# Tap matmuls on quarters of the array and half of the E transposes moved in a decoder trunk kernel

## The reference

```
h = x + 1/2 * SwiGLU_1(norm(x))
z = norm(h) @ W_in            # 2048 columns: 1536 for the conv heads, 512 for the S5 heads
y_a = B * causal_depthwise_conv3(C * v)
y_s = GLU(Re(C_bar state) + D * u_s)   # 32 channel groups of 16, a 64-dim complex diagonal state each
h = h + W_out(concat[norm(y_a), norm(y_s)])
h = h + 1/2 * SwiGLU_2(norm(h))
h = h + (p @ W_ple) * sigmoid(norm(h) @ W_gate)
```

```
kc[32*s + c_in, b, c_out] = sum over states of Er[state, b, s, c_in] * Gr[state, b, 0, c_out] + Ei * Gi
```

## Time and profile before

| | |
|---|---|
| median of 3 runs | 1042.67 us |
| the runs | 1042.33, 1049.44, 1042.67 us |
| profiled execution | 1048.33 us |
| its span, first to last instruction | 1046.5 us |
| its mean granted TensorE clock | 0.991 |
| busy: TensorE, VectorE, ScalarE, GpSimd | 1032.0, 658.3, 523.5, 364.6 us |
| tap matmuls (L1564, L1565) | 128 instructions in two layers |
| transposes of E (L1660) | 64 instructions in two layers |

### The profile page before, as it was taken

How to read it: one execution, slowest core, us unless ns; L and a number is a source line. 1 busy time by engine, 2 the same in 40 slices (tenths; PEclk the granted TensorE clock), 3 DMA queues, 4 the chain that set the end, 5 groups by cost and what they waited for, 6 DMA issues and landing times.

```text
span 1046.5 us, 15114 instructions
## 1 busy us (share of the span) xinstructions
PE 1032.0 (99%) x5345; PEld 882.1 (84%) x5345; DVE 658.3 (63%) x776; ACT 523.5 (50%) x736; POOL 364.6 (35%) x573
## 2 busy tenths in 40 slices
PE   8999999999999999999999999999999999999996
PEld 6888888899988888888788888889999888888885
DVE  5555665689876546655767545545897855455465
ACT  5544444575754444444664444444667444434454
POOL 6888999600137889940019400001002000000001
PEclk9999999999999999999999999997999999999999
DMA  9865555423457755553646655551334466556541
GB/s 278 247 197 174 191 191 172 160 81 130 145 165 187 260 174 187 189 197 136 201 162 200 200 181 181 199 188 54 121 122 161 157 207 198 185 177 199 189 150 44
DMA packets 143419, 181.56 MB, mean 173 GB/s; under 512 B 18384, under 2 KB 125584, under 8 KB 143376
## 3 DMA queue, kind: packets, MB, share of 16 engines
q1 hardware_dynamic: 143088, 180.48, 52.5%
q10 hardware_dynamic: 288, 0.52, 0.1%
HBM read 179.93 MB, written 1.05 MB: 173 GB/s over the span
## 4 chain that ended last, share of the span: by engine, by line
PE 97%; DVE 1%; ACT 1%; issue 0%; POOL 0%; POOLq 0%; ACTq 0%; DVEq 0%
PE ps L1426 29%; PE ps L1428 29%; PE ps L1427 29%; PE ps L1549 2%; PE ps L1443 1%; PE ps L1565 1%; PE ps L1564 1%; PE ps L1682 1%; PE ps L1696 1%; PE ps L1695 1%; PE ps L1681 1%; PE ps L1694 1%; PE ps L1660 1%; DVE wL L786 0%; ACT wH L419 0%
## 5 line engine op out<-in xcount | busy, mean ns | idle before, releaser
L786 DVE TENSOR_TENSOR wL<-raw,wH 128x1024 fp32r<-128x1024 f32 x336 | 423.5, 1302 | 129.3 <-ACT wH L419 129.2
L419 ACT ACTIVATE wH<-raw 128x1024 fp32r<-128x1024 f32 x336 | 335.9, 1052 | 126.2 <-PE ps L1428 121.6
L1426 PE MATMUL ps<-wH,uH 128*128 128x512 f32 x832 | 329.9, 396 | 3.7 <-DVE wL L786 2.5
L1428 PE MATMUL ps<-wH,uL 128*128 128x512 f32 x832 | 324.5, 390 | 0.0
L1427 PE MATMUL ps<-wL,uH 128*128 128x512 f32 x832 | 324.1, 390 | 0.0
L1426 PEld LDWEIGHTS ps<-wH,uH 128*128 128x128 f32 x832 | 156.3, 188 | 36.9 <-DVE uL L813 3.1
L1428 PEld LDWEIGHTS ps<-wH,uL 128*128 128x128 f32 x832 | 156.2, 188 | 33.3
L1427 PEld LDWEIGHTS ps<-wL,uH 128*128 128x128 f32 x832 | 156.5, 188 | 30.4
L1426 PE MATMUL ps<-wH,hTH 128*128 128x512 f32 x352 | 137.7, 391 | 0.0
L1428 PE MATMUL ps<-wH,hTL 128*128 128x512 f32 x352 | 137.4, 390 | 0.0
L1427 PE MATMUL ps<-wL,hTH 128*128 128x512 f32 x352 | 137.0, 389 | 0.0
(11 more groups left out here) (177 smaller groups left out, 1175.7 us busy)
## 6 DMA issues: line engine op xcount, KB each, us to landing
raw<-in_ffn_w_down_dram SPq DMA_DIRECT2D x88, 512.0 KB, 3.9
raw<-in_ffn_w_gate_dram SPq DMA_DIRECT2D x86, 512.0 KB, 4.0
raw<-in_ffn_w_up_dram SPq DMA_DIRECT2D x86, 512.0 KB, 5.0
raw<-in_w_in_dram SPq DMA_DIRECT2D x32, 512.0 KB, 4.3
raw<-in_w_out_dram SPq DMA_DIRECT2D x16, 512.0 KB, 4.2
raw<-in_ple_w_gate_dram SPq DMA_DIRECT2D x16, 512.0 KB, 4.0
raw<-in_glu_w_dram SPq DMA_DIRECT2D x4, 512.0 KB, 3.7
raw<-in_ple_w_proj_dram SPq DMA_DIRECT2D x4, 512.0 KB, 3.7
```

Source lines behind the costliest of these rows:

```text
L419: nc.scalar.activation(wH[:, slot, w], raw[:, slot, w], ACT.Copy).then_inc(wh_done, 1)
L786: nc.vector.tensor_tensor(wL[:, slot, w], raw[:, slot, w], wH[:, slot, w].bitcast(F32), ALU.subtract).then_inc((wl_half, wl_done)[a], 1)
L1426: mul(o, sH, vH, start=start, stop=False)
L1428: return mul(o, sL, vH, start=False, stop=stop)
```

## The change

1. The taps are computed with the operands swapped. `tap_round` makes G (32 columns) the stationary tile and streams the 128 columns of E. The output of block b = 4r + j goes to partitions 32j to 32j + 31 of PSUM bank 0, columns 128r to 128r + 127, so four matmuls in a row use four different quarters of 32 columns of the array. ScalarE copies the 512 columns to `kc` (semaphores `kt_ps`, `kt_done`), four transposes (`turn_taps`) turn them into bank 1, and ScalarE copies them to `kc` again, now in the layout that the rest of the kernel uses.
2. The turned E uses banks 6, 7, 2, 3. Two of the four groups of Er are turned ahead of x's tile 1, two behind it, and all 16 transposes of Ei come behind W_in unit 0.
3. W_in units 0 and 1 wait for the two copies of the taps (banks 0 and 1) instead of the E copies.
4. VectorE writes the second half of the low part of U_IN+1 after the norm, and the gains of tile 1 come behind its first E copy.

```
+E_BANKS = (6, 7, 2, 3)
...
+        kcf = kc[:].rearrange("p b c -> p (b c)")
...
-                act.wait_ge(kc_ps, l + 1)
-                nc.scalar.activation(kc[:], ps[:, 7, :].rearrange("p (b c) -> p b c", b=NB), ACT.Copy).then_inc(kc_done, 1)
+                act.wait_ge(kt_ps, l + 1)
+                nc.scalar.activation(kcf, ps[:, 0, :], ACT.Copy).then_inc(kt_done, 1)
                 E_turned(l, 0, 0)
                 norm_H(l, 1, 2)
                 norm_H(l, 1, 3)
+                act.wait_ge(kc_ps, l + 1)
+                nc.scalar.activation(kcf, ps[:, 1, :], ACT.Copy).then_inc(kc_done, 1)
                 E_turned(l, 0, 2)
                 E_turned(l, 1, 0)
                 E_turned(l, 1, 2)
...
-                split_at(l, U_IN + 1)
+                half_split(l, U_IN + 1, (U_IN + 1) % SLOTS, 0)
                 half_norm(l, 1, 0)
-                for h in range(2):
-                    gained(l, 1, 2 + h)
                 E_turned(l, 0, 1)
-                for h in range(2):
-                    rest(l, 1, 2 + h)
+                half_norm(l, 1, 1)
+                half_split(l, U_IN + 1, (U_IN + 1) % SLOTS, 1)
                 E_turned(l, 0, 3)
                 E_turned(l, 1, 1)
                 E_turned(l, 1, 3)
...
+            def tap_round(l, r):
+
+                for n, (gains, tables) in enumerate(((Gr, Er), (Gi, Ei))):
+                    for j in range(4):
+                        b = 4 * r + j
+                        last = mul(ps[32 * j:32 * j + 32, 0, P * r:P * r + P], gains[:, b, 0, :],
+                                   tables[:, b, :, :].rearrange("p s c -> p (s c)"), start=n == 0, stop=n == 1)
+                if r == 3:
+                    last.then_inc(kt_ps, 1)
+
+            def turn_taps(l):
+
+                pe.wait_ge(kt_done, l + 1)
+                for r in range(4):
+                    last = nc.tensor.transpose(ps[:, 1, P * r:P * r + P], kcf[:, P * r:P * r + P], ident[:])
+                last.then_inc(kc_ps, 1)
...
-                if j == 0:
-                    pe.wait_ge(et_done, l * 4 + 3)
-                if j == 1:
-                    pe.wait_ge(etd_done, l * 4 + 3)
+                if j < 2:
+                    pe.wait_ge((kt_done, kc_done)[j], l + 1)
...
-                for b in range(8):
-                    tap_block(l, b)
+                tap_round(l, 0)
+                tap_round(l, 1)
                 turn_x(l, 1, 0)
                 turn_x(l, 1, 1)
-                for b in range(8, NB):
-                    tap_block(l, b)
+                tap_round(l, 2)
+                tap_round(l, 3)
+                turn_E(l, 0, 0)
+                turn_E(l, 0, 1)
                 turn_x(l, 1, 2)
                 turn_x(l, 1, 3)
-                turn_E(l, 0)
-                turn_E(l, 1)
+                turn_taps(l)
+                for b in range(2, 4):
+                    turn_E(l, 0, b)
                 w_in_unit(l, 0)
+                for b in range(4):
+                    turn_E(l, 1, b)
                 w_in_unit(l, 1, lambda: drive(0))
```

More of the change, by code:

```diff
@@ L210, in trunk @@
         etd_done = sem("etd_done")
+        kt_ps, kt_done = sem("kt_ps"), sem("kt_done")
         kc_ps, kc_done, kc_full, taps_done = sem("kc_ps"), sem("kc_done"), sem("kc_full"), sem("taps_done")
@@ L491, in E_turned @@
                 nc.scalar.activation((ETr, ETi)[r][:, 4 * b:4 * b + 4, :],
-                                     ps[:, SIDE_BANKS[b], :].rearrange("p (b c) -> p b c", b=4),
+                                     ps[:, E_BANKS[b], :].rearrange("p (b c) -> p b c", b=4),
                                      ACT.Copy).then_inc(et_done, 1)
@@ L860, in E_turned @@
                 nc.vector.tensor_copy((ETr, ETi)[r][:, 4 * b:4 * b + 4, :],
-                                      ps[:, SIDE_BANKS[b], :].rearrange("p (b c) -> p b c", b=4)).then_inc(etd_done, 1)
+                                      ps[:, E_BANKS[b], :].rearrange("p (b c) -> p b c", b=4)).then_inc(etd_done, 1)
             def hidden(l, f, i, between=None):
@@ L1648, in w_in_unit, with turn_E @@
                 last.then_inc(wt_used, 1)
[L1650 to L1662, removed]
+            def turn_E(l, r, b):
+                if r == 1 and b in EA:
+                    pe.wait_ge(et_done, l * 4 + (b // 2 + 1))
+                elif r == 1:
+                    pe.wait_ge(etd_done, l * 4 + (b // 2 + 1))
+                elif b == 2:
+                    pe.wait_ge(tg_done, l * 16 + 6)
+                for j in range(4):
+                    last = nc.tensor.transpose(ps[:, E_BANKS[b], j * P:(j + 1) * P],
+                                               (Er, Ei)[r][:, 4 * b + j, :, :].rearrange("p s c -> p (s c)"), ident[:])
+                last.then_inc(et_ps, 1)
             def stats(l, k):
```

## The result

The changed kernel takes 1053.69 us (median of 12 runs, 1052.06 to 1055.12), the kernel before 1048.49 (median of 12 runs, 1042.33 to 1049.82): ratio 1.0054, 95% interval 1.0037 to 1.0072. It is slower, by less than 1%. The profiled execution took 1053.72 us with a span of 1051.9.

What follows compares the result with a forecast made beforehand. TensorE, busy 99% of the span, was taken to bound the kernel. From the profiled 1048.33 us: plus 2 x 1.85 for later drives, minus 5.8 for layer 1's clock fall, plus 1.5 for a new fall, 1047.7; range 1042 to 1053.

Steps and rivals of the forecast that it cites:

- What bounds the kernel now: Whole kernel: TensorE bounds it, busy 99% of the span; a clock fall in layer 1's mixer entry cost 5.8 us.
- Part 1: Tap matmuls at the mixer entry: 7.0 us a layer removed, 3.4 added, so 3.6 us less tap work.
- Part 2: Start of W_in unit 0 in layer 0: 208.5 us instead of 212.0, 3.5 us earlier.
- Part 3: Moved E transposes delay drive_in(0): TensorE waits 3.5 us in unit 1, drive(0) starts 1.85 us later a layer.
- Rival (b): Ahead of drive(0): no wait, as VectorE and ScalarE finish sooner; -1.7 us a layer, 1039.1 us; chance 0.10.
- (a): Tap matmuls: the array's quarters do not overlap; +4.8 us a layer, 1052.1 us; chance 0.18.
- Part 4: Clock behind the wait ahead of drive(0): one fall in the two layers, priced at 1.5 us.
- rival (c): Both layers' mixers: clock stays down long, from quarter-array matmuls or the wait over drive(0); 1057.8 us; chance 0.10.
- The prediction's own sign: Changed profile, either layer: the forecast falls if the granted clock is low for more than 5 us.

Runs made afterwards that it cites:

- e6: Changed kernel with all Ei transposes back ahead of unit 0 and a round's eight tap matmuls in one quarter of the array; 1042.75 us, ratio to before 0.996.
- e4: Changed kernel with the eight tap matmuls of a round all in one quarter of the array instead of four in turn; 1059.41 us, ratio to before 1.011.
- e7: On top of e2, the first four E groups go into the gaps ahead of x's tiles 0 and 1; 1035.38 us, ratio to before 0.9892.
- e1: Changed kernel with drive_in(0) ahead of the split of U_IN+2 on VectorE and ScalarE; 1040.23 us, ratio to before 0.9926.
- e2: Changed kernel with all 16 Ei transposes back ahead of unit 0, quarter-array taps kept; 1037.24 us, ratio to before 0.9896.
- e3: Changed kernel with 14 identity matmuls as filler on TensorE ahead of its wait for drive_in(0); 1045.81 us, ratio to before 0.9976.
- e8: Changed kernel with drive(0) moved behind the second half of unit 1, TensorE's wait staying in the middle of unit 1; 1051.44 us, ratio to before 1.0048.

## Why the prediction was wrong, by its own steps

The forecast was 1047.7 with a range of 1042 to 1053; the time is 1053.7, just outside. It is slower, as forecast, against either median, by 0.5% against that of twelve runs and by 1.06% against the 1042.67 of three. That the ratio of 1.0054 agrees with the forecast 0.5% is luck: the forecast counted from 1042.67, and from there it has 5.0 us where 11.0 were measured. The error in the time and the higher median of before cancel.

**What bounds the kernel now: right, with one wrong inference.** The fall in layer 1 was read rightly, and its price of 5.8 us too: the runs of before without a fall are at 1042.4. But "the median of 1042.67 is a run without a fall" was true of the three runs, of which two have none, and not of the kernel. The forecast time does not rest on it, but its percentage does. It also hid that a kernel which only avoids before's falls wins 5.5 us on the median, as e6 does (1042.75 against 1048.29).

**Part 1, taps: the term was mis-sized and it did not matter.** 3.4 us a layer was taken, 1.7 measured (27 ns spacing, the lower bound). The stated reason, that both instructions of a matmul stand together in one quarter's queue, does not hold: the quarters ran fully side by side, which e4 shows by taking them away. As predicted, the saving ends in a wait for the scaled x, of 1.02 us where 0.5 was reckoned.

**Part 2, unit 0: right.** 208.5 predicted, 208.35 measured. That the norm chain sets this time e7 shows, where unit 0 starts 0.1 us behind the last low part.

**Part 3, the queues: right.** A wait of 3.5 us and drive(0) at 222.55 were predicted, 3.35 us and 222.30 measured. e1 (order of the queues) and e2 (place of the transposes) each remove it, 13.5 and 16.5 us faster. Without falls the sum gives 1046.2; e3 measures 1045.8. Rival (b), no wait, is out by the 3.35 us, and (a), no overlap, by the 27 ns.

**Part 4, the clock: the step that failed.** It put one fall in the two layers at a quarter of 5.8 us, 1.5 in all. There were two, worth 7.9 together (e3): 4.8 and 3.2 by the timeline. The 6.4 us between 1.5 and 7.9 account for the miss of 6.0. The reason given for the low price was "Behind this wait comes dense f32r work", and that was wrong in this kernel's own order: behind the wait comes drive(0) first, 32 plain f32 instructions with 64 columns each. The clock was low over all of it in layer 0 and over all but the first 1.2 us in layer 1. e8 tries the premise: with f32r work right behind the wait a fall costs 1.5 to 2 us, near the 1.5 that was taken. So the size was wrong for this order of the queue, and the number of falls was too low. This was the second half of rival (c), the wait that drops the clock and keeps it down over drive(0), at two thirds of its price of 11.6 us; its first half, that matmuls on a quarter of the array do not hold the clock, is ruled out by e1 and e2. Rival (c) was to decide once two falls cost 3.4 us each, and they cost 3.9. It had a chance of 0.10, and the range left it out. The prediction's own sign, a granted clock that is low for more than 5 us in a layer, came true in both (10.2 and 6.8 us). What sets how long a fall lasts is shown only as far as e8 goes.

## What to carry to other kernels

When work on the bounding engine is moved behind a stage, write down what the helpers' queues hold behind the copies that this work releases: here 1.8 us of moved transposes held up a split and a copy that the next stage needed, and turned a 3.65 us gain into a 1.6 us loss. A wait of 3.4 us on TensorE had a second price here, in the clock, where one of 0.54 us (e1) had none; nothing between was tried. That price went by what followed the wait: 3.2 to 4.8 us with drive(0) behind it, 1.5 to 2 with f32r matmuls. So look at what stands behind a wait, and price it at 1.2 GHz. And take a kernel's base from many runs before reading small differences: the runs of this one lie at 1042.4, 1045.1, 1048.3 and 1049.8, and two at 1053.4.

## What was not expected of the hardware

- Plain f32 matmuls with 32 stationary columns in four quarters of the array start 27 ns apart at 128 moving columns, against 109 ns in one quarter and 109 ns for 128 stationary columns with 32 moving.
- The granted clock fell on tap matmuls of 32 moving columns while the engine was busy in all of the microsecond (before, layer 1, 713 to 714), and none of ten runs shows a fall in its time or mean clock where the taps took the same time with 128 moving columns (e6). Busy time in the profile does not tell whether the clock will hold.
- Fourteen identity matmuls (28 instructions) in a 3.4 us wait kept the clock up, and are worth 7.9 us in two places.
